# Convolution products and a Fourier transform inside a differential-attention stream, and square sums inside the next product, in a four-layer kernel on one core

## The reference, cut to what matters

```python
# layer 0: the queries and keys, normalized per head of 64, then rotated
q_x, k_x, v_x = jnp.split(h_x @ w_qkv, [qd, qd + kvd], axis=-1)
q_x = rope_2d(rms_norm(q_x.reshape(B, S, N_HEADS, HEAD_DIM), q_gain), tables)
k_x = rope_2d(rms_norm(k_x.reshape(B, S, N_KV_HEADS, HEAD_DIM), k_gain), tables)
# layers 2 and 3: four groups of 256 columns of the mixed output
z = h @ w_in
mixer_b = group(z, G_BB) * dwconv3(group(z, G_BC) * group(z, G_BX), w)      # short convolution
mixer_c = jnp.fft.fft2(f, axes=(1, 3), norm='ortho').real                   # Fourier transform
a = softmax(q1 @ k1.T) - lam * softmax(q2 @ k2.T)                           # differential attention
mix = jnp.concatenate([mixer_a, mixer_b, mixer_c, rmsnorm(a @ v, g) * (1 - lam_init)], axis=-1)
x = x + gt1 * (mix @ w_out)
```

## Time and profile before

| what | value |
|---|---|
| three runs | 3591.99, 3592.34, 3600.01 us; median 3592.34 us |
| profiled execution | 3596.15 us, of which the span from first to last instruction is 3594.8 us |
| TensorE busy | 3384.1 us, 94% of the span |
| VectorE, ScalarE, GpSimd busy | 50%, 35%, 7% of the span |
| mean granted TensorE clock | 0.962 of 2.4 GHz |

### The profile page before, as it was taken

The page is one execution under the profiler, slowest core; times in us unless marked ns, Lnnn a source line. Parts: engine busy times, 40 slices in busy tenths (PEclk is TensorE's granted clock), DMA queues, the critical chain, the costliest instruction groups (busy, mean ns, idle before and its releaser), DMA issues.

```text
span 3594.8 us, 43191 instructions
## 1 busy us (share of the span) xinstructions
PE 3384.1 (94%) x18016; PEld 2798.3 (78%) x18016; DVE 1790.4 (50%) x2721; ACT 1255.0 (35%) x1781; POOL 247.6 (7%) x329
## 2 busy tenths in 40 slices
PE   6979989999989999989999999889999989889998
PEld 3767778888877877868887885778888878568886
DVE  3567455334345445457574336366435443744343
ACT  4357442112234324253232425342112243543232
POOL 1111110000100000010002000100000100010001
PEclk7989999999999999999999998899999999889999
DMA  6400134323211211225453210123323222012222
GB/s 237 160 25 2 30 111 133 126 83 129 87 67 48 96 62 58 85 71 185 160 182 117 91 65 1 36 106 129 129 83 125 90 93 82 1 59 95 97 97 88
DMA packets 87779, 334.28 MB, mean 93 GB/s; under 512 B 11168, under 2 KB 14240, under 8 KB 83744
## 3 DMA queue, kind: packets, MB, share of 16 engines
q1 hardware_dynamic: 66416, 252.85, 20.1%
q0 software_dynamic: 21168, 78.65, 6.7%
HBM read 329.37 MB, written 2.10 MB: 92 GB/s over the span
## 4 chain that ended last, share of the span: by engine, by line
PE 90%; DVE 4%; ACT 4%; issue 1%; DMA 0%; POOL 0%; SPq 0%; DVEq 0%; ACTq 0%; POOLq 0%
PE PS L344 67%; PE PS L370 6%; PE PS L357 3%; PE PS L558 3%; PE PS L536 2%; PE PS L630 1%; PE PS L481 1%; PE PS L494 1%; PE PS L655 1%; PE PS L470 1%; PE PS L526 1%; PE PS L601 1%; PE PS L642 1%; DVE dP L1536 1%; ACT aPT L850 1%
## 5 line engine op out<-in xcount | busy, mean ns | idle before, releaser
L703 ACT ACTIVATE WH<-WR 128x1024 fp32r<-128x1024 f32 (+1 forms) x376 | 418.8, 1114 | 1573.6 <-PE PS L344 1370.6
L344 PE MATMUL PS<-HH,WH 128*128 128x512 f32 (+1 forms) x3104 | 940.5, 357 | 24.6 <-DVE HL L1513 11.0
L344 PE MATMUL PS<-HL,WH 128*128 128x512 f32 (+1 forms) x3104 | 936.2, 356 | 0.0
L344 PE MATMUL PS<-HH,WL 128*128 128x512 f32 (+1 forms) x3104 | 934.7, 355 | 0.0
L1075 DVE TENSOR_TENSOR WL<-WR,WH 128x1024 fp32r<-128x1024 f32 (+1 forms) x376 | 486.0, 1293 | 848.4 <-ACT WH L703 848.0
L344 PEld LDWEIGHTS PS<-HH,WH 128*128 128x128 f32 x3104 | 513.8, 189 | 114.5 <-DVE HL L1513 12.7
L344 PEld LDWEIGHTS PS<-HH,WL 128*128 128x128 f32 x3104 | 513.7, 189 | 86.0
L344 PEld LDWEIGHTS PS<-HL,WH 128*128 128x128 f32 x3104 | 513.3, 189 | 85.7 <-issue 1.2
L344 PE MATMUL PS<-DH,WH 128*128 128x512 f32 (+1 forms) x1056 | 319.0, 356 | 0.0
L344 PE MATMUL PS<-DH,WL 128*128 128x512 f32 (+1 forms) x1056 | 318.6, 356 | 0.0
L344 PE MATMUL PS<-DL,WH 128*128 128x512 f32 (+1 forms) x1056 | 318.5, 356 | 0.0
(11 more groups left out here) (269 smaller groups left out, 3812.5 us busy)
## 6 DMA issues: line engine op xcount, KB each, us to landing
WR<-in_win SPq DMA_DIRECT2D x176, 512.0 KB, 3.5
AT<-in_adat POOLq DMA_DIRECT2D x144, 512.0 KB, 3.8
WR<-in_wdn SPq DMA_DIRECT2D x64, 704.0 KB, 4.0
WR<-in_wret SPq DMA_DIRECT2D x64, 512.0 KB, 3.3
WR<-in_zin SPq DMA_DIRECT2D x36, 512.0 KB, 3.5
AR<-in_ada SPq DMA_DIRECT2D x8, 1024.0 KB, 11.5
aV<-in_ada SPq DMA_DIRECT2D x8, 1024.0 KB, 4.9
aAR<-in_ada SPq DMA_DIRECT2D x8, 1024.0 KB, 6.5
```

The lines of the kernel that those rows point to most:

```text
L344: mm = PE.matmul(dst[:, a:b], w[u % 2][:, k * P:(k + 1) * P], h[:, k, a:b], start=(k == 0 and i == 0), stop=(k == nk - 1 and i == 2))
L703: AC.activation(M.WH[u % 2][:, 0:n], M.WR[u % 2][:, 0:n], COPY).then_inc(*on.up("w_hi", u))
```

## The change

Layer 0: the two key units come first (QK is the order of the units), and the square sum of a unit, with `ada_turn`, is issued inside the next product (after two or three of its tiles) in place of after its own. The last ones go into the value rows. The rotation's product on GpSimd goes to VectorE, `aKF` gives way to spare room in aQ, the queries for the scores are stacked before the value rows end, and the value rows are packed in three banks and copied by ScalarE alone.

Layers 2 and 3: the six convolution units, in parts of two or three tiles (PACE steps to a unit), and then the Fourier transform, are issued inside the steps of the attention loop: scores, values, part of a unit or of the transform, transposes. All six units go through one pair of banks (PS3), and the attention's values share PS2 with its transposes. The transposed probabilities have three buffers in place of four. ScalarE's and VectorE's work for the units, for the convolution and for the transform's splits is spread over the same steps. Three of four parts of the 512-token transform matrix are loaded late, into rooms that the convolution and the last unit leave. `project` starts with a `product_pair`, with the square sums after three tiles of it.

```diff
--- before.py
+++ after.py
+QK = (8, 9, 0, 1, 2, 3, 4, 5, 6, 7)
+V_PLACES = (0, 1, 2)
...
+PACE = {2: 3, 3: 2}
...
-                    ("mix_lo", l) if l and n == 0 else None, between if n == 0 else None)
+        if l:
+            product_pair(u, PS, segs, ("mix_lo", l), between)
+        for n in range(2 * (l > 0), KT):
+            product(u + n, PS[n % 2], (HH, HL), KT, segs, ("x_out", (l, n - 2)) if n > 1 else None)
...
+        def square_sum(p):
+            PE.wait_ge(*on("q_squared", QK[p]))
+            PE.wait_ge(*on("rms", ("q", QK[p - 1])) if p else on("table", "attention"))
             for a, b, _ in ALL:
                 mm = PE.matmul(PS[2][:, a:b], M.aBD[:, :], M.aSQ[:, a:b], start=True, stop=True)
-            mm.then_inc(*on.up("q_square_sum", n))
...
+        def beside(p, at, squares_at, turn_at):
+
+            if at == squares_at and p != 1:
+                square_sum(p)
+            if at == turn_at and p > 1:
+                ada_turn(0, A0 + QK[p], M.aKF)
+
+        product_pair(u, PS, ALL, ("h_lo", "0a"))
+        for p in range(2, 10):
+            last = p - 1 if p > 2 else 0
+            product(u + p, PS[p % 2], (HH, HL), KT, ALL, ("q_squared", QK[p - 2]) if p > 3 else None, None,
+                    lambda k: beside(last, k, 3 if p == 3 else 2, 5))
+            if p == 2:
+                square_sum(1)
+            ada_sum(0, A0 + QK[p], buf, (0, A0 + QK[p] - 1))
         for half in range(2):
-            product_rows(u + 10 + half, 4, 4 * half, L, range(6), lambda m: bank(PS, m)[:, 0:L], half == 0, half == 1)
-
-        PE.wait_ge(*on("aV_odd", 5))
-        PE.wait_ge(*on("aV", 4))
+            product_rows(u + 10 + half, 4, 4 * half, L, range(6), lambda m: v_place(PS, m), half == 0, half == 1, None, True,
+                         (lambda m: ("v_rows", m // 2) if m in (1, 3) else None) if half else None,
+                         None if half else lambda at: beside(9, at, 6, 14))
+
+        PE.wait_ge(*on("aV", 1))
...
+            product_rows(u + 2 + ROWS_AT + v, 4, 4 * v, L, range(6), place, v == 0, v == 1, None, True)
+
+        pace = PACE[l]
+
+        def convolved(step):
+
+            i, part = divmod(step, pace)
+            un = u + mix_place(ROWS_AT + i)
+            if part == 0:
+                PE.wait_ge(*on("w_lo", un))
+                PE.wait_ge(*(on("z_copied", (l, MIX[ROWS_AT + i - 1])) if i else on("dv_copied", (l, 2))))
+            product_tiles(un, PS[3], range(KT * part // pace, KT * (part + 1) // pace), segs)
...
+        def fourier(step):
+
+            if step == 0:
+                for m in range(2):
+                    features(m, ("z_copied", (l, MIX[-1])))
+            elif step == 1:
+                for m in (2, 3):
+                    features(m, ("dft_copied", (l, m - 2)))
+            elif step in (2, 3):
+                for m in (2, 3):
+                    PE.wait_ge(*on("dft_copied", (l, m)))
+                PE.wait_ge(*on("dft", (l, 0)))
+                PE.wait_ge(*on("dft", (l, 1)))
+                tokens(step - 2, 0, lambda q, m: M.CN[2 * q + m // 2][:, m % 2, :], 4, S)
+            elif step == 4 and n > S:
+                for m in (4, 5):
...
+                out = PS[2][:, T + (h // 2) * P:T + (h // 2 + 1) * P]
                 for m in range(nm):
                     for g in range(2):
                         mm = PE.matmul(out[64 * g:64 * g + 64, :], M.DV[:, m0 + m, 64 * (h + g):64 * (h + g) + 64],
-                                       M.dPT[(j + g) % 4][:, m, :], start=(m == 0), stop=(m == nm - 1))
+                                       M.dPT[(j + g) % 3][:, m, :], start=(m == 0), stop=(m == nm - 1))
                 mm.then_inc(*on.up("d_values", (l, j // 2)))
-
-        def square_sums():
-            for t in range(2):
+            if step < 6 * pace:
+                convolved(step)
+            else:
+                fourier(step - 6 * pace)
+            j = step - 2
+            if 0 <= j < len(heads):
+                PE.wait_ge(*on("d_prob", (l, j)))
+                PE.wait_ge(*(on("d_turned", (l, j - 1)) if j else on("dv_copied", (l, 1))))
+                if j > 3 and j % 4 == 0:
+                    PE.wait_ge(*on("d_out", (l, heads[j - 4][0])))
+                for m in range(heads[j][2]):
+                    mm = PE.transpose(PS[2][:, m * P:(m + 1) * P], M.dP[0][j % 3][:, m * P:(m + 1) * P], M.dID[:, :])
+                mm.then_inc(*on.up("d_transposed", (l, j)))
+        def square_sums(k):
+            for t in range(2 if k == 3 else 0):
                 PE.wait_ge(*on("o_squared", (l, t)))
-                PE.wait_ge(*on("d_turned", (l, len(heads) - 1)))
+                PE.wait_ge(*(on("mix_lo", (l, 5)) if t else on("d_out", (l, heads[-1][0]))))
                 for a, b, _ in segs:
                     mm = PE.matmul(PS[2 + t][:, a:b], M.dBD[:, :], (M.dP[0][0], M.dP[0][1])[t][:, a:b], start=True, stop=True)
...
+        def z_copy(p):
+
+            un, z = u + mix_place(p), MIX[p]
+            refill(un + 2)
+            AC.wait_ge(*on("product", un))
+            dst, w = (Z[:, z, 0:n], n) if z < 12 else (M.DK[:, z - 12, :], T)
+            AC.activation(dst, PS[p % 2 if p < ROWS_AT else 3][:, 0:w], GELU if z < 2 else COPY).then_inc(*on.up("z_copied", (l, z)))
+
...
-                              COPY).then_inc(*on.up("d_out", (l, q)))
+            if step < 6 * pace and step % pace == pace - 1:
+                z_copy(ROWS_AT + step // pace)
+            if step in (2 * pace, 5 * pace):
+                middle(step // (3 * pace))
+            if step >= 6 * pace:
...
+            VE.tensor_tensor(dst, raw[:, 0:S], M.aT2[:, :], ALU.add).then_inc(*on.up("rope", n))
+            if p in (3, 4):
+                key_low(p - 3)
...
+            if 0 < at <= 6 * pace and at % pace == 0:
+                refill(u + mix_place(ROWS_AT + at // pace - 1) + 2)
+            for v in range(2):
+                if at in (pace * (3 * v + 2), pace * (3 * v + 2) + 1):
+                    conv(v, at - pace * (3 * v + 2))
+                if at == pace * (3 * v + 3):
+                    conv(v, 2)
+            fourier(at - 6 * pace)
         N = [*M.dP[0], M.dP[1][0]]
         for t in range(2):
...
-        PO.wait_ge(*on("table", "attention"))
-        for n in range(10):
-            PO.wait_ge(*on("q_normed", n))
-            PO.tensor_tensor(M.aSQ[:, 0:S], M.aRAW[n % 2][:, 0:S], M.aCOS[:, :], ALU.mult).then_inc(*on.up("q_t1", n))
         PO.wait_ge(*on("aSK", 0))
...
-        SP.dma_start(M.CN[:, :, :, :], dram["dft512"]).then_inc(*on.up("dft", (l, 0), 16))
+        SP.dma_start(M.CN[0][:, :, :], dram["dft512"][:, 0, 0:2, :]).then_inc(*on.up("dft", (l, 0), 16))
         u = FIRST["zin", l]
         for n in range(18):
             load(u + n + 2)
+        SP.wait_ge(*on("conv_product", (l, 1)))
+        for i in (1, 2):
+            SP.dma_start(M.CN[i][:, :, :], dram["dft512"][:, i // 2, 2 * (i % 2):2 * (i % 2) + 2, :]).then_inc(*on.up("dft", (l, 1), 16))
+        SP.wait_ge(*on("product", u + 17))
+        SP.dma_start(M.CN[3][:, :, :], dram["dft512"][:, 1, 2:4, :]).then_inc(*on.up("dft", (l, 1), 16))
         if l == 2:
-            SP.wait_ge(*on("product", u + 17))
-            SP.dma_start(M.CC[:, :, :, :], dram["dft256"].rearrange("p q (m k) -> p q m k", m=2)).then_inc(*on.up("dft", (l, 1), 16))
+            SP.dma_start(M.CC[:, :, :, :], dram["dft256"].rearrange("p q (m k) -> p q m k", m=2)).then_inc(*on.up("dft_ctx", l, 16))
```

More of the change, by code:

```diff
@@ L176, in attention @@
         self.top = top
[L177 removed]
+        self.aQS = [QS0, t("aQS1", [P, 16, P], F32R)]
         self.aP = [t(f"aP{i}", [P, NB]) for i in range(4)]
@@ L329, in tensor_program, with product @@
     PS, HH, HL, WH, WL = M.PS, M.HH, M.HL, M.WH, M.WL
-    def product(u, dst, src, nk, segs, after=None, ready=None, between=None, place=3):
+    def product(u, dst, src, nk, segs, after=None, ready=None, between=None):
         PE.wait_ge(*on("w_lo", u))
@@ L337, in product @@
         for k in range(nk):
-            if between and k == place:
-                between()
+            if between:
+                between(k)
             if ready:
@@ L346, in product, with product_tiles, product_pair @@
         mm.then_inc(*on.up("product", u))
-    def product_pair(u, dst, segs, ready):
+    def product_tiles(u, dst, tiles, segs):
+        for k in tiles:
+            for i, (w, h) in enumerate(((WH, HH), (WH, HL), (WL, HH))):
+                for a, b, _ in segs:
+                    mm = PE.matmul(dst[:, a:b], w[u % 2][:, k * P:(k + 1) * P], h[:, k, a:b],
+                                   start=(k == 0 and i == 0), stop=(k == KT - 1 and i == 2))
+        if k == KT - 1:
+            mm.then_inc(*on.up("product", u))
+    def product_pair(u, dst, segs, ready, between=None):
         for v in range(2):
@@ L360, in product_pair, with product_rows @@
                     mm.then_inc(*on.up("product", u + v))
```

(18 more changed lines are left out.)

417 lines of the change are left out of this document (197 added, 220 removed).

## The result

| | us | ratio to before |
|---|---|---|
| before | 3592.16 (3591.98 to 3600.01) | |
| after | 3512.03 (3508.49 to 3515.66, 4 runs) | 0.9772 [0.9755, 0.9789] |

A forecast was written before the change was run, and what follows sets the result against it. TensorE holds 90% of the chain of waits, so gains come only where it stands still or runs at half clock. Terms 27.6 + 23.3 + 20.7 + 8.2 = 79.8 us less gave 3512 to 3513 us, range 3488 to 3545.

The forecast's parts named there:

- layer 0: From the first key pair to the first scores: 128.4 us against 154.0, plus 2.0 of clock, 27.6 less (bounds 12 and 33.3).
- layer 2's loop: Value rows to last values in layer 2: work 136.7 plus waits 13.7 us, 23.3 less (bounds 10 and 33).
- layer 3's loop: The same stretch in layer 3: 111.3 us against 132.0, 20.7 less (bounds 12 and 29).
- pair of project: First products of project: third unit earlier by 5.1 us in layer 2, 3.1 in layer 3, together 8.2 (bounds 3 and 12).
- Layer 0's clock: Layer 0: work counted at full clock, and no clock fall at the scores after a 2.3 us gap, 2.0 us more gain.
- The hand-overs in the loop: Layer 2's attention loop: 0.3 us in each of 18 steps for hand-overs and half-clock moments, 5.4 in all; at most 18.
- Rival 1: Attention loops of layers 2 and 3 paced by latencies, losing 1.0 us a step as now: 3534 us, chance 0.14.
- Rival 2: Units and transform inside the attention loops run at half clock, doubling their time: 3638 us, chance 0.05.
- the rule beside it: Trainium skill: matmul groups cycling through banks with small idle moments keep falling to the lower clock; in the loops, 3638 us.
- Rival 3: Layer 0: single aSQ chains the units, every product stands 2 us; gain 12 there, whole 64: 3528 us, chance 0.06.
- Rival 4: More comes back: hand-overs near nothing, all loop time at full clock, gains 98 or more: 3490 us, chance 0.08.
- rival 5: A wait in a fixed queue blocks the stream, so the change has no effect: within 10 us of before, chance 0.05.

The follow-up runs named there:

- The filler: Kernel before, with six unused 128x256 matmuls after the transposes of each attention step from the fifth on, layers 2 and 3: 3594.04 us, ratio 0.9993.
- the three moves: Changed kernel with layer 2's middle convolution image a step later, project's square sums earlier, layer 0's third unit's weights split first: 3503.97 us, ratio 0.9749.

## Why the prediction was right, step by step

| term | predicted | measured | how |
|---|---|---|---|
| layer 0 | 27.6 | 24.8 | next common product at 371.60 for 396.76, less 0.4 that lies before the pair |
| layer 2's loop | 23.3 | 26.1 | 147.6 for 173.7 |
| layer 3's loop | 20.7 | 21.9 | 110.1 for 132.0 |
| pair of project | 8.2 | 7.7 | loop end to end of the products: 75.5 for 80.6, 50.8 for 53.4 |
| sum | 79.8 | 80.5 | the medians differ by 80.1 |

The sum is right partly because two errors of 3 us have opposite signs. That is luck, and so is part of the agreement of 80.5 with 80.1: the two profiled executions, from which the table is measured, differ by 85.7, and the other 5.2 lie in stretches with the same instructions.

- **Layer 0's work and first waits** hold: 2.8 us for the third product's weights (3.2 predicted), 0.4 (0.3) and 1.5 (1.9) for the square sums of the third and fourth product, 2.2 (2.3) for ScalarE's copy ahead of the scores, and no wait in steady state. That sum of 7.7 came to 6.9.
- **Layer 0's clock** is the term that was mis-sized. The prediction counted the third product at full clock and 2.0 us back at the scores. After the wait of 2.8 us the clock is 0.85 in the next 11.2 us, which is some 3.3 us at half clock, and 1.7 us lost; the scores still ran at 0.80 over 8.5 us. The pair is followed by the scores 130.3 us later, not 128.4: with 0.8 less of waits and 1.7 lost to the clock some 1.0 is left that I cannot place. The run with the weights split first takes the wait to 1.66 us (on ScalarE's square) and has clock 1.00 in the same window.
- **The hand-overs in the loop**, called the unknown, were put at 0.3 us in each of 18 steps. They are near nothing: in the window of 87.2 us TensorE is busy for 85.0, a step takes 5.97 us (6.3 predicted). The Fourier steps and the end of the loop were put at 6.9 us of waits and have 4.4 (idle from 2180.60). Against that stand the 4.0 us of the wait on dPT and the half clock behind it, which no term had; the text named the mechanism (copies held up on ScalarE) only as what could make it wrong, and had the units' copies hold them up, where it was the convolution's.
- **Layer 3** holds: 110.1 for 111.3, since its steps of 5.99 us have no such wait (5.0 us in eight waits, the longest 1.6).
- **The pair**: third unit 24.3 us after the loop for 23.8, and 17.9 for 17.6. The last tile was ready 20.2 us after the loop, as counted. The new wait for WL is shorter than 2.5 (0.57 and 1.79). In layer 2 that is no gain: the last tile ran at half clock (from 2237.69 two matmuls start every 0.64 us, ahead of the wait for it every 0.35), and what it lost the wait had less.
- **Rival 1** (1.0 us a step) is excluded by the same window. **Rival 2** (units at half clock) and the rule beside it: the clock is 1.00 over 87.2 us and 0.97 in layer 3's. The Trainium skill (TensorE: Matmul & The Clock Gate, "A second HAM failure mode: psum-queue depth-cycling") has grouped matmuls with small idle moments fall back to the lower clock; this trace does not agree for steps that hold a part of a unit, though the heads alone went back and forth between the two levels, as it says (0.90 and 0.73). **Rival 3** (one aSQ chains the units) is wrong, 92.5 of 94.4 us being busy. **Rival 4**'s condition came true in the loop's main part (hand-overs near nothing, clock 1.00), its size did not; **rival 5** is excluded by the time.

What was only argued: that all of layer 2's 26 us come from covered waits. The filler shows room in the middle heads, but the higher clock made a part of it, and in layer 3 some 3 us of the added matmuls were paid. How the 26 us divide between covered waits and matmuls that no longer run at half clock is not shown. The units without the transform give 13 of them; why the transform needs the units ahead of it is read from windows, not tested by itself.

## What to carry to other kernels

A loop of small matmuls that looks slow by its clock may be slow by its latencies: put unused matmuls into it, and if the time stays, count that room as what can be filled, less what the added matmuls gave back by raising the clock. Fill every step of such a loop rather than its first ones, since bare steps at the end give back what full ones gained. When side work goes into a stream, look on every engine at what is queued behind an instruction that waits for another engine; here one step's delay of such an instruction and an earlier start of two square sums brought some 9 us more in layer 2. And follow an earlier start to the end of its stretch: two of the four that were won here were lost again to half clock.

## What was not expected of the hardware

- A loop whose TensorE was busy for 44.6 of 49 us took nearly 8 us of further matmuls (0.71 in each step) without getting longer. A part of that busy time was half clock and matmuls behind each other, so a busy share of 91% was no sign of a full engine.
- Which stand costs the clock could not be read off its length: after 2.83 us (layer 0) and 2.75 us (layer 2) matmuls ran at half clock, after 2.48 us in layer 3 they did not; with the three moves two stands of 1.50 and 1.79 us there were followed by some 3 us in which a matmul started every 0.43 us in place of 0.23.
- The same feed-forward instructions, with TensorE busy all through and clock 1.00, took 532.79 us in the profile before, 535.98 in the one after and 532.79 again in the repeat of the changed kernel. Differences of 3 us between two profiles of this kernel are thus no effect of an edit.
